# A chunked scan that works on two chunks at once: the inverse of one, the state of the one before

## What is computed

```python
w_log = -softplus(-(w0 + tanh(zw) @ w2)) - 0.5
decay = exp(-exp(w_log))
def step(S, inp):                       # S (heads, v, k)
    r_t, w_t, k_t, v_t, kk_t, b_t = inp
    sa = -einsum("bhvk,bhk->bhv", S, kk_t)
    S = S * w_t + sa[..., None] * b_t + v_t[..., None] * k_t
    return S, einsum("bhvk,bhk->bhv", S, r_t)
s_fwd_c, y_fwd_c = rwkv_scan(zero, fc, 0, reverse=False)   # context
s_bwd_c, y_bwd_c = rwkv_scan(zero, fc, 1, reverse=True)
_, y_fwd_x = rwkv_scan(s_fwd_c, fx, 0, reverse=False)      # latent tokens
_, y_bwd_x = rwkv_scan(s_bwd_c, fx, 1, reverse=True)
```

## Time and profile before

| | us |
|---|---|
| median of 3 runs | 2168.02 (2167.54 to 2170.58) |
| the profiled execution | 2174.26 |
| its span, first to last instruction | 2172.5 |
| scan of layer 0, first to last matmul | 225.2 |
| scan of layer 1, first to last matmul | 210.5 |
| PE busy in the span | 89% |
| DVE, ACT, POOL busy in the span | 47%, 35%, 14% |

### The profile page before, as it was taken

The page is one execution under the profiler, slowest core; times in us unless marked ns, Lnnn a source line. Parts: engine busy times, 40 slices in busy tenths (PEclk is TensorE's granted clock), DMA queues, the critical chain, the costliest instruction groups (busy, mean ns, idle before and its releaser), DMA issues. The chain is left out here.

```text
span 2172.5 us, 51547 instructions
## 1 busy us (share of the span) xinstructions
PE 1937.1 (89%) x22829; PEld 1559.0 (72%) x22829; DVE 1027.4 (47%) x1713; ACT 751.7 (35%) x1380; POOL 297.9 (14%) x381
## 2 busy tenths in 40 slices
PE   4986888889889999899998998958888889998988
PEld 1671788854568888678886676838787558988988
DVE  1545666562643333443332124566666363545544
ACT  0324333323542222232222113354333453435432
POOL 2102433301100111010001001034331110100000
PEclk8997999999999999999999998979999999999999
DMA  8513000010112323223234851200001114554543
GB/s 322 180 36 145 5 4 5 4 52 22 40 61 68 106 89 97 78 88 107 87 107 178 308 193 57 85 1 5 5 5 44 32 40 150 183 165 155 175 147 126
DMA packets 143452, 203.96 MB, mean 94 GB/s; under 512 B 6718, under 2 KB 123672, under 8 KB 137088
## 3 DMA queue, kind: packets, MB, share of 16 engines
q1 hardware_dynamic: 141728, 198.96, 27.3%
q0 software_dynamic: 1504, 1.71, 0.2%
HBM read 199.61 MB, written 1.05 MB: 92 GB/s over the span
## 5 line engine op out<-in xcount | busy, mean ns | idle before, releaser
L330 DVE TENSOR_TENSOR W_low<-RING,W_high 128x1024 fp32r<-128x1024 f32 x268 | 329.4, 1232 | 461.2 <-ACT W_high L327 460.7
L366 PE MATMUL BANK<-H_high,W_high 128*128 128x512 f32 (+2 forms) x1472 | 511.8, 348 | 19.9 <-ACT H_high L632 9.6
L367 PE MATMUL BANK<-H_low,W_high 128*128 128x512 f32 (+2 forms) x1472 | 507.9, 345 | 0.0
L368 PE MATMUL BANK<-H_high,W_low 128*128 128x512 f32 (+2 forms) x1472 | 507.5, 345 | 0.0
L327 ACT ACTIVATE W_high<-RING 128x1024 fp32r<-128x1024 f32 x268 | 281.1, 1052 | 594.4 <-PE BANK L368 572.2
L366 PEld LDWEIGHTS BANK<-H_high,W_high 128*128 128x128 f32 (+1 forms) x1472 | 279.9, 190 | 65.2 <-issue 27.6
L368 PEld LDWEIGHTS BANK<-H_high,W_low 128*128 128x128 f32 (+1 forms) x1472 | 280.0, 190 | 34.4
L367 PEld LDWEIGHTS BANK<-H_low,W_high 128*128 128x128 f32 (+1 forms) x1472 | 280.1, 190 | 33.9 <-issue 0.6
L1275 PE MATMUL BANK<-RING,WORK 64*64 64x64 f32 x4352 | 162.4, 222 | 14.3 <-issue 8.5
L1275 PEld LDWEIGHTS BANK<-RING,WORK 64*64 64x64 f32 x4352 | 144.6, 134 | 27.1 <-issue 10.4
L366 PE MATMUL BANK<-hidden_high,W_high 128*128 128x512 f32 (+1 forms) x352 | 122.9, 349 | 12.0 <-PEq L2188 12.0
(11 more groups left out here) (307 smaller groups left out, 2825.4 us busy)
## 6 DMA issues: line engine op xcount, KB each, us to landing
RING<-w_in_dram SPq DMA_DIRECT2D x46, 1024.0 KB, 5.5
RING<-w_ffn_in_dram SPq DMA_DIRECT2D x44, 1024.0 KB, 5.1
lation_weights_ffn<-w_mod_dram SPq DMA_DIRECT2D x24, 1024.0 KB, 6.2
RING<-w_ffn_out_dram SPq DMA_DIRECT2D x20, 1024.0 KB, 5.1
tion_weights_opening<-w_mod_dram SPq DMA_DIRECT2D x8, 1024.0 KB, 8.5
ulation_weights_norm<-w_mod_dram SPq DMA_DIRECT2D x8, 1024.0 KB, 6.8
on_weights_features<-w_mod_dram SPq DMA_DIRECT2D x8, 1024.0 KB, 5.0
RING<-w_out_dram SPq DMA_DIRECT2D x8, 1024.0 KB, 5.1
```

The lines of the kernel that those rows point to most:

```text
L330: low_ready.mark(nc.vector.tensor_tensor(self.part(1, c), self.raw(c), self.part(0, c).bitcast(FP32), ALU.subtract))
L366: nc.tensor.matmul(out, w[0], x[0], start=start, stop=False)
L367: nc.tensor.matmul(out, w[0], x[1], start=False, stop=False)
L368: return nc.tensor.matmul(out, w[1], x[0], start=False, stop=stop)
```

## The change

The state part of a chunk moves into the next chunk's inverse. `run` now makes 9 rounds: round i inverts chunk i (for i < 8) and works on the state of chunk i - 1 (for i > 0). All that the state part needs of its chunk exists twice and is used by turns (QR, T2, GRAM_X, BK_TOK, V_X, ARB), so `keep` goes. The w and sa products move from banks B_L and B_LT to B_S, and WS gets a buffer of its own. PE's hand-written order becomes:

```diff
-    (grams, levels 1 to 5 with v turns and the first ds products,
-     then w, y, w, y, sa, y, ds)
+    grams(i)
+    x1(1); v_turn(0); tx(1); v_turn(1)
+    x1(2); w_begin(); tx(2); w_end(); y_begin()
+    x1(3); y_middle(); tx(3); sa(0); sa(1)
+    x1(4); y_end(0); tx(4); y_end(1); ds_begin(0)
+    x1(5); ds_begin(1); ds_end(0); tx(5); ds_end(1)
```

The first round has no state part, the ninth only that, in the order w, y, w, y, sa, sa, ds_begin twice, y_end and ds_end by direction. Waits that come in on PE:

```diff
 def wide(d):
-    if need_y:
-        pe.wait_ge(*at_step(s_y_out[d], i - y0))
+    pe.wait_ge(*at_step(s_t[d], i, LEVELS))
+    if i > 0 and reads(i - 2):
+        pe.wait_ge(*at_step(s_y_out[d], i - 1 - y0))
...
+def w_begin():
+    for d in range(NDIR):
+        pe.wait_ge(*at_step(s_st[d], s))
+        pe.wait_ge(*at_step(s_v_tok[d], s, 1, 1))
+        pe.wait_ge(*at_step(s_gram_out[d], s, 1, 1))
+        if inverse:
+            pe.wait_ge(*at_step(s_v_tok[d], i, 1, 1))
...
+def y_begin():
+    ...
+                pe.wait_ge(*at_step(s_gram_out[d], i, 1, 1))
```

DVE's order in a round:

```diff
+if inverse:
+    begin(0); begin(1); gram_out(0); gram_out(1)
+    for l in range(1, LEVELS - 1):
+        merge_level(l, 0); merge_level(l, 1)
+        if more and l == 1:
+            exponents(i + 1)
+        if more and l >= 3:
+            operands(i + 1, l - 3)
+if s is not None:
+    new_state(0)
+if inverse:
+    merge_level(NL, 0); merge_level(NL, 1)
+if s is not None:
+    if reads(s):
+        add_y(0); add_y(1)
+    new_state(1)
```

```diff
-                for d in range(NDIR):
-                    for j in range(PAIRS):
-                        pool.wait_ge(*scaled(PAIRS * d + j + 1))
-                        nc.gpsimd.tensor_tensor(EXCL[d][:, j], INCL[d][:, j], EXCL[d][:, j], ALU.subtract)
...
-    nc.scalar.activation(e[:, 0], excl, ACT.Exp, scale=-KAPPA)
-    nc.scalar.activation(e[:, 1], incl, ACT.Exp, scale=-KAPPA)
-    s_exp.mark(nc.scalar.activation(e[:, 2], incl, ACT.Exp, scale=KAPPA))
+    if d == 0:
+        incl = INCL[0][:, :, bass.ds(chunk_of(0, i), CHUNK)]
+        nc.scalar.activation(SHRINK[0][:, :, 1:], incl, ACT.Exp, scale=-KAPPA)
+        s_exp.mark(nc.scalar.activation(GROW[0], incl, ACT.Exp, scale=KAPPA))
+    else:
+        nc.scalar.activation(SHRINK[1], TO_END, ACT.Exp, scale=-KAPPA)
+        s_exp.mark(nc.scalar.activation(GROW[1], TO_END[:, :, 0:HD], ACT.Exp, scale=KAPPA))
```

More of the change, by code:

```diff
@@ L1065, in _, with operands @@
             def _(pool):
[L1066 removed]
+                def operands(i, d):
                     pool.wait_ge(*at_step(s_gram[d], i, 4))
@@ L1071, in operands, with step @@
                     pool.wait_ge(*at_step(s_exp, i, 2, d + 1))
[L1072 to L1075 removed]
+                    s_ops[d].mark(nc.gpsimd.tensor_tensor(BK[d][:, :, 1], KD[d][:, :, bass.ds(chunk_of(d, i), CHUNK)], GROW[d], ALU.mult))
+                def step(i, inverse, s, more):
+                    if not inverse:
+                        return
                     for l in range(1, LEVELS):
@@ L1113, in bk_token_major, with step @@
+                def step(i, inverse, s, more):
                     def bk_token_major(d):
                         act.wait_ge(*at_step(s_bk_turned[d], i, 1, 1))
[L1116 to L1122, removed]
-                        s_lts[d].mark(nc.scalar.activation(LTS[d], BANK[:, 4 * d + B_LT].rearrange("p (j q t) -> p j q t", j=PAIRS, q=2)[:, :, 0], ACT.Copy))
@@ L1254, in _ @@
             def _(pe):
-                def each(bank, at, width, lhs, rhs, stride=None):
-                    stride = stride or width
-                    for j in range(PAIRS):
-                        for rows in (UP, DOWN):
-                            last = nc.tensor.matmul(BANK[rows, bank, at + j * stride:at + j * stride + width],
-                                                    lhs(j)[rows], rhs(j)[rows], start=True, stop=True)
-                    return last
                 OWN, OTHER = (UP, DOWN), (DOWN, UP)
@@ new lines, in ds_end @@
+                    def ds_end(d):
+                        pe.wait_ge(*at_step(s_ds_1[d], s, 1, 1))
+                        s_ds[d].mark(side_by_side(HD, (4 * d + B_S, 0, STAY, lambda j: BK_TOK[d][c][:, 0, j], lambda j: SA[d][:, j], False, True))[0])
+                    if inverse and s is None:
+                        grams(i)
+                        x1(1)
+                        v_turn(0)
+                        tx(1)
+                        x1(2)
+                        v_turn(1)
+                        tx(2)
+                        for l in range(3, LEVELS):
+                            x1(l)
+                            tx(l)
+                    elif inverse:
+                        grams(i)
+                        x1(1)
+                        v_turn(0)
+                        tx(1)
+                        v_turn(1)
+                        x1(2)
+                        w_begin()
+                        tx(2)
+                        w_end()
+                        y_begin()
+                        x1(3)
+                        y_middle()
+                        tx(3)
+                        sa(0)
+                        sa(1)
+                        x1(4)
+                        y_end(0)
+                        tx(4)
+                        y_end(1)
+                        ds_begin(0)
+                        x1(5)
+                        ds_begin(1)
+                        ds_end(0)
+                        tx(5)
+                        ds_end(1)
+                    else:
+                        w_begin()
+                        y_begin()
+                        w_end()
+                        y_middle()
+                        sa(0)
+                        sa(1)
+                        ds_begin(0)
+                        ds_begin(1)
+                        y_end(0)
+                        ds_end(0)
+                        y_end(1)
+                        ds_end(1)
```

383 lines of the change are left out of this document (196 added, 187 removed).

## The result

| | before | after |
|---|---|---|
| median, on one chip by turns (20 runs each) | 2169.51 us (2162.21 to 2181.15) | 2177.02 us (2170.04 to 2182.28) |
| ratio, 95% interval | | 1.0033 (1.0019 to 1.0046) |
| span of the profiled execution | 2172.5 us | 2176.5 us |
| scan of layer 0, first to last matmul | 225.1 us | 224.2 us |
| scan of layer 1 | 210.4 us | 212.9 us |

The change costs 7.5 us, 0.33%. The forecast was 2169, with 2163 to 2174 as its own range and 2147 to 2180 as the whole one; the time lies in the whole range, 3 us above the forecast's own, and on the slower side, to which the prediction gave 0.26.

What follows compares the result with a forecast made beforehand. The prediction took the arrival of PE's instructions to bound the scans. Terms -2.4 + 1.0 - 0.6 + 3.0 = +1.0 gave 2174.3 + 1.0 - 6.2 = 2169 us; own range 2163 to 2174, whole range 2147 to 2180.

Steps and rivals of the forecast that it cites:

- The bound: Both scans: paced by the arrival of PE's instruction blocks, about 3.8 us each, not by the chain of waits.
- Less idle for ACT and DVE: Both scans: a listed sign that the forecast is right, ACT and DVE standing idle for less time.
- boundary rival: Between rounds: DVE's state, merges and y-sums idle PE besides the fetch; 2184 us, half the price 2177; chance 0.17.
- the wait at `wide`: Next round's wide product waits for DVE's last merge and y-sum; 0 to +13.6 us, taken as +1.0.
- The same products in another order: Both scans: same PE instruction count, less time above the stall spacing; -1.2 to -3.5 us, taken as -2.4.
- The start: Start of each scan: first operands wait for two exponentials instead of three; -0.3 us a scan.
- The end: Ninth round: PE waits for DVE's state, then does the state part alone; taken as +1.5 us a scan.
- The work beside the path: Removed copies, exponential and subtractions on DVE, ACT and POOL run while PE waits for code; 0 us.
- Chain: Both scans: the chain of waits sets the time, overlap gains 1.6 us a round; 2151 us, chance 0.24.
- No overlap: Scans: a bank wait holds the state part until the inverse is done, only ends count; +2.4 us, 2170, chance 0.05.

Runs made afterwards that it cites:

- the kernel that does this part alone: Kernel before without exclusive sums: two exponentials for three, one DVE subtraction for two, no POOL subtractions in `features`; 2174.78 us, 1.0003.
- the halved pair: Kernel before and changed kernel, each with half of PE's scan instructions at the same streamed columns: 2117.45 us (0.9722) and 2070.11 us (0.9507).
- joined products: Changed kernel with states written early in the last inverse round and each direction's two turning products made one: 2177.96 us, 1.0038.
- the kernel with both states together: Changed kernel; in the last inverse round PE closes both ds sums earlier and DVE writes both states before last merges and y sums: 2176.29 us, 1.0008.
- mending the ends: Changed kernel with the whole ds sum of the last inverse round brought forward and both states written between merge levels 3 and 4: 2174.53 us, 1.0001.

## Why the prediction was right, and where it was off

**The bound** was read rightly. 59 and 56 packets, about 3.8 us a block from stall to stall and more idle time at "issue" came as listed. "Less idle for ACT and DVE" did not hold in layer 0, where PE's waits for DVE behind the start rose from 4.6 to 9.0 us, by the wait for the state and the one at `wide`. Halving PE's instructions at the same columns then took 31 and 26 us off the scans of the kernel before. The layer 0 scan (224.2) is in its range of 222 to 228, layer 1's (212.9) in 207 to 214. The Trainium skill, "Runtime: NRT & Kernel Launch", Instruction fetch mechanics, has the cost of crossing a block as mostly hidden. The trace disagrees: in the changed kernel 33 and 34 us of a scan go by "issue".

**The range.** The forecast's sum was +1.0 us and its own range ended at 2174; the change measured +7.5, 2177.02 us. Only the whole range holds that, and its upper part was there for another theory: half the boundary rival's price gave 2177. The runs make that agreement chance, as the wait at `wide` cost 1 to 2 us and not 7.

**The same products in another order**, -2.4, and **the wait at `wide`**, +1.0, together -1.4. From the first matmul to the instruction from which the ends are measured above, layer 0 went from 215.4 to 211.3 us and layer 1 from 200.9 to 200.8: -4.2 together, which is within what one execution of a scan varies by. The wait came as described, behind DVE's line, but for 1.0 us by the row and in five rounds, where I had 1.4 in eight and 0.4 in six. The blocks with it took 4.2 to 4.4 us, where I had 4.0. It was half as frequent, and net of what the next block gave back its price of 1.2 us is near the 1.0 that I took.

**The start**, -0.3 a scan, came as foreseen: PE's wait ahead of the first matmul fell from 14.1 to 13.8 us in layer 0 and from 14.5 to 14.2 in layer 1.

**The end**, +1.5 a scan, is the term that was too small. The wait was right (2.9 us foreseen; 3.0 and 2.5 in the rows above). The state part was not: 6.0 us foreseen, 8.0 and 8.5 measured. PE ran it at a low granted clock: the window rows above show 0.72 and 0.62 in layer 0, 0.62 and 0.80 in layer 1, where the rounds' windows show 1.00, and where the kernel before kept 1.00 to the end of its scans. In layer 0 the clock fell to 0.50 (1.2 GHz) at 435.2, while PE stood idle, and stayed there to 442.0, 4.7 us of the 8.0; in layer 1 it was 4.4 us of the 8.5, without the stall in it. An estimate: had PE done that work in half the time, the state parts would have taken 5.7 and 6.3 us, about what was foreseen. By the prediction's own sum, 2.9 + 8.0 - 6.9 is 4.0, not 2.0. The ends measured +3.2 and +2.6, +5.8 for both scans instead of +3.0. The prediction had the bound of 2.0 "or 3 with a stall on top" and took a value below both; it gave the end the price of a loop at full clock.

**The work beside the path** at 0: confirmed by the kernel that does this part alone (1.0003).

**The rivals.** *Chain*: wrong for the full code, and right about the overlap once half the code is gone. Its price was too small: the halved pair shows 20 us a scan, some 3 us a round, where the prediction had 1.6. Part of that is in its own sum: four gaps of 0.77 us take 3.1 of the 4.74 us of products and leave 1.7, not 2.7, which makes 2.6 us a round; the rival's time would then have been 2137 us. *Boundary*: present and cheap. *No overlap*: refuted by the halved pair.

**What stays open.** -4.2 and +5.8 make +1.6 in the two scans (-0.9 and +2.5), and the starts take 0.5 off that, while the medians differ by 7.5 and the two spans by 4.0. The rest is not located. One execution of a scan varies by up to 5 us, and the time outside the two scans lay between 1734 and 1742 us in the profiled executions of full-code kernels with unjoined products and no transposes, so two profiles cannot hold the difference exactly. The profiled execution of the kernel with both states together even had longer scans (226.9 and 213.1 us) than the changed kernel beside it (224.2 and 214.1), with its ends 3.6 us shorter. That mending the ends takes the ratio from 1.003 to 1.000 says that most of the loss belongs there, and not more than that.

## What to carry to other kernels

When an engine stands still for nothing that the profile names, and does so after equal counts of its own instructions, count instructions before waits: here shortening the chain of waits bought nothing, and the cover that it used up came back as a bill where the pipeline drains. A pipelined loop has one more end than the loop it replaces; cost that end with the clock that its idle time brings, not with the clock of the loop. Fewer instructions only pay if the ones that are left are no slower: look at the spacing of the new form, and at the waits that it moves, before trading count for it.

## What the runs showed of the hardware

- PE's code came in blocks of some 253 recorded instructions each 3.7 to 3.8 us in the mean (single blocks of the changed kernel from 3.3 to 4.2), in scans in which the DMA engines were busy for 2% of the time. A block that took 4.41 us, with the wait at `wide` late in it, ended without a stall; one of 4.20 us with that wait at its start ended in a stall of 1.18 us, and one of 5.17 us with joined products in one of 0.38. What sets the moment at which the next block is asked for is open.
- With PE idle for 1.1 to 3.4 us ahead of or in the ninth round, the granted clock fell to 0.50 in that idle time or within 1 us behind it, in both scans of all five profiled executions of the changed kernel and its variants with another end or DVE order. In the kernel before, which has no such wait, it stood at 1.00 to the end of both scans.
- Ordinary float32 matmuls and transposes by turns run one after the other, a group of two matmuls and the transpose behind it at a spacing of 0.43 us at granted clock 1.00. Over the layer 0 scan the granted clock was 0.86 with the transposes and 0.93 without, and 0.76 in the changed kernel with them.
- Float32 weights of 64 rows by 128 columns came at 56 ns a matmul; 64x64 products side by side at 15 ns.
